# Cross attention of a deep block: split-precision products, transposed queries, shares scaled on VectorE

## What is computed

```python
def cross_attention(h, mm, wq, wk, wv, wo):
    q = (h @ wq).reshape(B, S, XA_HEADS, XA_HEAD_DIM)
    k = (mm @ wk).reshape(B, M, XA_HEADS, XA_HEAD_DIM)
    v = (mm @ wv).reshape(B, M, XA_HEADS, XA_HEAD_DIM)
    s = jnp.einsum('bshd,bmhd->bhsm', q, k) * (XA_HEAD_DIM ** -0.5)
    p = jax.nn.softmax(s, axis=-1)
    o = jnp.einsum('bhsm,bmhd->bshd', p, v).reshape(B, S, D_MODEL)
    return o @ wo
```

## Time and profile before

| | |
|---|---|
| median of 3 runs | 1783.58 us (1782.58 to 1783.75) |
| profiled execution | 1782.28 us, of which 1780.5 us lie between first and last instruction |
| PE busy | 97% of the span |
| DVE, ACT, POOL busy | 62%, 50%, 10% |
| mean granted PE clock | 0.995 of 2.4 GHz |

### The profile page before, as it was taken

How to read it: one execution, slowest core, us unless ns; L and a number is a source line. 1 busy time by engine, 2 the same in 40 slices (tenths; PEclk the granted TensorE clock), 3 DMA queues, 4 the chain that set the end, 5 groups by cost and what they waited for, 6 DMA issues and landing times.

```text
span 1780.5 us, 22807 instructions
## 1 busy us (share of the span) xinstructions
PE 1735.2 (97%) x9317; PEld 1473.0 (83%) x9317; DVE 1105.6 (62%) x1327; ACT 890.3 (50%) x1040; POOL 184.5 (10%) x142
## 2 busy tenths in 40 slices
PE   8989999999999999999999999999999999999997
PEld 6787999978878787999888878888888887888886
DVE  7867655568767754655556775565555667565554
ACT  6555544465556554544455445544445544654442
POOL 1100000014352241000021000000003000000000
PEclk9999999999999999999999999999999999999999
DMA  8426555555535526555565464465556456446551
GB/s 292 168 95 213 172 185 191 188 140 189 166 96 184 170 96 207 174 189 188 189 211 166 145 233 168 128 201 188 188 169 198 149 206 213 142 144 200 189 189 71
DMA packets 160791, 311.07 MB, mean 175 GB/s; under 512 B 5851, under 2 KB 53472, under 8 KB 159920
## 3 DMA queue, kind: packets, MB, share of 16 engines
q1 hardware_dynamic: 158512, 299.33, 50.7%
q0 software_dynamic: 2176, 10.29, 1.6%
HBM read 304.35 MB, written 5.24 MB: 174 GB/s over the span
## 4 chain that ended last, share of the span: by engine, by line
PE 83%; DVE 8%; ACT 5%; issue 2%; DMA 1%; POOL 1%; SPq 0%; DVEq 0%; ACTq 0%; POOLq 0%
PE ps L458 22%; PE ps L460 22%; PE ps L459 22%; PE ps L663 4%; PE ps L662 4%; PE ps L661 4%; PE ps L421 3%; DVE wlo L1447 3%; ACT whi L956 2%; DVE ps L1596 1%; PE ps L875 1%; ACT work L1053 1%; PE ps L891 1%; DMA raw<-in_a_w_qkv 1%; DMA sums<-st 1%
## 5 line engine op out<-in xcount | busy, mean ns | idle before, releaser
L1447 DVE TENSOR_TENSOR wlo<-raw,whi 128x2048 fp32r<-128x2048 f32 x279 | 643.3, 2309 | 435.8 <-ACT whi L956 426.6
L458 PE MATMUL ps<-whi,hT_hi 128*128 128x512 f32 x1936 | 765.4, 395 | 9.1 <-DVE hT_lo L1474 2.5
L460 PE MATMUL ps<-whi,hT_lo 128*128 128x512 f32 x1936 | 752.6, 389 | 0.0
L459 PE MATMUL ps<-wlo,hT_hi 128*128 128x512 f32 x1936 | 751.5, 388 | 0.0
L956 ACT ACTIVATE whi<-raw 128x2048 fp32r<-128x2048 f32 x279 | 533.8, 1914 | 361.8 <-PE ps L460 305.0
L458 PEld LDWEIGHTS ps<-whi,hT_hi 128*128 128x128 f32 x1936 | 364.4, 188 | 88.0 <-issue 10.8
L460 PEld LDWEIGHTS ps<-whi,hT_lo 128*128 128x128 f32 x1936 | 364.0, 188 | 76.2
L459 PEld LDWEIGHTS ps<-wlo,hT_hi 128*128 128x128 f32 x1936 | 364.7, 188 | 70.2
L661 PE MATMUL ps<-hT_hi,whi 128*128 128x256 f32 x640 | 182.8, 286 | 1.7 <-ACT work L1114 0.9
L662 PE MATMUL ps<-hT_lo,whi 128*128 128x256 f32 x640 | 181.5, 284 | 0.0
L663 PE MATMUL ps<-hT_hi,wlo 128*128 128x256 f32 x640 | 181.4, 283 | 0.0
(11 more groups left out here) (202 smaller groups left out, 1061.0 us busy)
## 6 DMA issues: line engine op xcount, KB each, us to landing
raw<-in_w_in SPq DMA_DIRECT2D x46, 1024.0 KB, 5.1
raw<-in_w SPq DMA_DIRECT2D x88, 512.0 KB, 4.6
raw<-in_m_w_up SPq DMA_DIRECT2D x32, 1024.0 KB, 5.2
raw<-in_m_w_down SPq DMA_DIRECT2D x32, 1024.0 KB, 4.8
raw<-in_kv_w SPq DMA_DIRECT2D x24, 1024.0 KB, 5.1
raw<-in_w SPq DMA_DIRECT2D x22, 1024.0 KB, 4.9
raw<-in_b_w_q SPq DMA_DIRECT2D x12, 1024.0 KB, 5.2
raw<-in_a_w_qkv SPq DMA_DIRECT2D x11, 1024.0 KB, 6.5
```

Of the source, the lines that this page charges most:

```text
L458: pe.matmul(acc, xh, wh, start=start and k == 0, stop=False)
L459: pe.matmul(acc, xh, wl, start=False, stop=False)
L460: ins = pe.matmul(acc, xl, wh, start=False, stop=stop and k == kc - 1)
L1447: vec.tensor_tensor(wlo[:, m % SPLIT, :], raw[:, m % RAW, :], whi[:, m % SPLIT, :], ALU.subtract).then_inc(*mark("lo_ready", ("lo", m)))
```

## The change

- The queries are projected by `up_chunk()`, transposed, without the row scale. ACT writes their rounded high part (`xq_hi`) and DVE the low part (`xq_lo`) straight from PSUM; `xa_turn_q` and the copies belonging to it go away. The row scale goes into the exponential instead: ACT takes it as `scale`, and DVE multiplies the maxima by its negative. DVE makes these two scale vectors after the row scale (two small products).
- The loaded keys and values are split into a high part (ACT, `memory_hi`, 128 x 2048) and a low part (DVE, `memory_lo`, the same size, in place). The keys' and the values' high parts and the keys' low part are written at the time of the product before (`w_o_2`), the values' low part in cross attention.
- Scores and values are three fp32r passes each in place of one fp32 matmul.
- The turned probabilities are split as well: `xp_hi` on ACT, `xp_lo` on DVE.
- DVE scales the exponentials itself (`xshare`: a reciprocal and two products of 128 x 256 a head); POOL does nothing here any more.
- On PE the scores of head 0 stand behind Q1, those of head 1 in the middle of Q2, the turn of head 0's probabilities behind Q2, values of head 0 and the turn of head 1 in the middle of Q3, and the values of head 1 and scores of heads 2 and 3 behind Q3. The rest keeps its place.

The core of the diff (declarations and walks shortened; eight leading blanks are cut):

```diff
-nat = sb("nat", [P, T, D])
+nat, nat_r = sb_twice("nat", [P, T, D])
...
-wide = sb("wide", [P, 2 * 3072])
+wide, wide_r = sb_twice("wide", [P, 2 * 3072])
...
-qn = pnf[:, 0:T * D].rearrange("p (t c) -> p t c", t=T)
-qT = pnf[:, T * D:T * D + KD * S].rearrange("p (k s) -> p k s", k=KD)
+q_hi, q_lo = [pn_r[:, KD * S * j:KD * S * (j + 1)].rearrange("p (k s) -> p k s", k=KD) for j in range(2)]
+k_hi = wide_r[:, 0:KD * S].rearrange("p (k s) -> p k s", k=KD)
+v_hi = wide_r[:, KD * S:KD * S + T * D].rearrange("p (t d) -> p t d", t=T)
+k_lo, v_lo = km_r.rearrange("p (k s) -> p k s", k=KD), vm_r.rearrange("p (t d) -> p t d", t=T)
...
-pxT = [pnf[:, 4608 + 512 * j:5120 + 512 * j].rearrange("p (m c) -> p m c", m=2) for j in range(2)]
+pT_hi = [pn_r[:, 4608 + 512 * j:5120 + 512 * j].rearrange("p (m c) -> p m c", m=2) for j in range(2)]
+pT_lo = [nat_r[:, 0, 512 * j:512 * j + 512].rearrange("p (m c) -> p m c", m=2) for j in range(2)]
...
         def xa_scores(h):
-            pe.wait_ge(*at("T free", uq_[h]))
+            pe.wait_ge(*at("q split", l, h))
             if h >= 2:
                 pe.wait_ge(*at("xexp", l, h - 2))
             elif h == 0:
-                pe.wait_ge(*at("merged", l, T - 1, 1))
-                pe.wait_ge(*at("mem back", l))
+                pe.wait_ge(*at("keys split", l))
             for t in range(T):
                 for k in range(2):
-                    ins = pe.matmul(ps[:, SC + h % 2, t * S:(t + 1) * S], qT[:, 2 * h + k, t * P:(t + 1) * P],
-                                    kmT[:, 2 * h + k, :], start=k == 0, stop=k == 1)
+                    acc = ps[:, SC + h % 2, t * S:(t + 1) * S]
+                    qh, ql = [q[:, 2 * h + k, t * P:(t + 1) * P] for q in (q_hi, q_lo)]
+                    kh, kl = [b[:, 2 * h + k, :] for b in (k_hi, k_lo)]
+                    pe.matmul(acc, qh, kh, start=k == 0, stop=False)
+                    pe.matmul(acc, qh, kl, start=False, stop=False)
+                    ins = pe.matmul(acc, ql, kh, start=False, stop=k == 1)
             ins.then_inc(*mark("scored", ("xscores", l, h)))
...
+            elif h == 0:
+                pe.wait_ge(*at("values split", l))
...
+                    acc = ps[:, OB + h % 2, j * S:(j + 1) * S]
+                    vh, vl = [b[:, k, d:d + P] for b in (v_hi, v_lo)]
+                    ph, pl = [b[h % 2][:, k, :] for b in (pT_hi, pT_lo)]
+                    pe.matmul(acc, vh, ph, start=k == 0, stop=False)
+                    pe.matmul(acc, vh, pl, start=False, stop=False)
+                    ins = pe.matmul(acc, vl, ph, start=False, stop=k == 1)
...
-        chunk(hT[0], tx[v + 1], early=lambda: x_half(v + 1, 1))
-        ch = c.ch
-        free = lambda t, half: ("acc free", ch - 1, t)
-        tile(hT[0], 0, ACCB, True, False, None, free, lambda: xa_scores(0), lambda: xa_turn_q(0))
-        xa_scores(1)
-        tile(hT[0], 4, ACCB, False, True, None, None, xa_middle, lambda: xa_turn_p(0))
-        c.ch += 1
-        xa_values(1)
-        xa_turn_q(1)
-        xa_scores(2)
-        xa_scores(3)
+        def xa_inside(n):
+            if n == 2:
+                xa_scores(1)
+            if n == 3:
+                xa_values(0)
+                xa_turn_p(1)
+
+        def xa_after(n):
+            if n == 1:
+                xa_scores(0)
+            if n == 2:
+                xa_turn_p(0)
+            if n == 3:
+                xa_values(1)
+                xa_scores(2)
+                xa_scores(3)
+
+        up_chunk(tx[v + 1], lambda: x_half(v + 1, 1), xa_after, 0, xa_inside)
+        up_chunk(None, None, xa_after, 2, xa_inside)
...
+        def memory_hi(to, loaded, name):
+            act.wait_ge(*at("mem back", l))
+            for t in range(T):
+                act.wait_ge(*at("merged", l, t, 1))
+            sc.activation(to, loaded, CP).then_inc(*mark("memory_hi", (name, l)))
+
+        tick()
+        tick()
+        c.ch += 1
+        memory_hi(k_hi, kmT, "keys hi")
+        tick()
+        memory_hi(v_hi, vm, "values hi")
+        tick()
+        c.ch += 1
+        x_half(v + 1, 0)
+
+        def xq_hi(h):
+            act.wait_ge(*at("acc", c.m - 1, h % 2, 0))
+            sc.activation(q_hi[:, 2 * h:2 * h + 2, :].rearrange("p k s -> p (k s)"), ps[:, ACC + h % 2, :], CP).then_inc(
+                *mark("q_hi", ("q hi", l, h)))
...
-            plain(pxT[h % 2].rearrange("p m c -> p (m c)"))
+            hi_of(pT_hi[h % 2].rearrange("p m c -> p (m c)"))
...
         begin(v + 1, junk2)
         tick()
-        out_of_acc(CP, lambda tt: qn[:, tt, 0:512], rs_of(v + 1))
-        tick()
-        xq_turn(0)
+        xq_hi(0)
+        xq_hi(1)
+        tick()
         xexps(0)
-        tick()
         xexps(1)
-        xp_turn(0)
+        tick()
+        xp_hi(0)
+        xq_hi(2)
         xo_hi(0)
-        xp_turn(1)
-        out_of_acc(CP, lambda tt: qn[:, tt, 512:1024], rs_of(v + 1))
+        xp_hi(1)
+        xq_hi(3)
+        c.ch += 2
         xo_hi(1)
-        xq_turn(1)
         tick()
         xexps(2)
         xexps(3)
-        xp_turn(2)
-        tick()
-        xp_turn(3)
+        xp_hi(2)
+        tick()
+        xp_hi(3)
         xo_hi(2)
         xo_hi(3)
...
+        def memory_lo(loaded, lo, hi, hi_key, key):
+            dve.wait_ge(*at(hi_key, l))
+            vec.tensor_tensor(lo, loaded, hi, ALU.subtract).then_inc(*mark("memory_lo", (key, l)))
+
+        tick()
+        tick()
+        add_chunk(v + 1, 0, c.m - 1)
+        memory_lo(kmT, k_lo, k_hi, "keys hi", "keys split")
+        tick()
+        last_to_x(v + 1)
+
+        def xq_lo(h):
+            dve.wait_ge(*at("q hi", l, h))
+            hi, lo = [b[:, 2 * h:2 * h + 2, :].rearrange("p k s -> p (k s)") for b in (q_hi, q_lo)]
+            vec.tensor_tensor(lo, ps[:, ACC + h % 2, :], hi, ALU.subtract).then_inc(*mark("q_split", ("q split", l, h)))
+            same[("acc free", c.ch, h % 2)] = ("q split", l, h)
+            c.ch += h % 2
+
+        def xp_lo(h):
+            c.tu = turned_at["xp", l, h]
+            if h >= 2:
+                dve.wait_ge(*at("xav", l, h - 2))
+            lo_of(pT_hi[h % 2].rearrange("p m c -> p (m c)"), pT_lo[h % 2].rearrange("p m c -> p (m c)"))
...
-            vec.tensor_scalar(mx[:, o:o + 2], big, -(256 ** -0.5), None, ALU.mult).then_inc(*mark("negmaxes", ("xnegmax", l, h)))
-
-        def xrec(h):
+            vec.tensor_tensor(mx[:, o:o + 2], big, rst[:, 6:8], ALU.mult).then_inc(*mark("negmaxes", ("xnegmax", l, h)))
+
+        def xshare(h):
             dve.wait_ge(*at("xexp", l, h))
-            vec.reciprocal(st[:, 16 + 2 * h:18 + 2 * h], st[:, 8 + 2 * h:10 + 2 * h]).then_inc(*mark("xrecs", ("xrec", l, h)))
+            rec = st[:, 16 + 2 * h:18 + 2 * h]
+            settle(dve, vec.reciprocal(rec, st[:, 8 + 2 * h:10 + 2 * h]), "xrecs", "xrec", l, h)
+            for t in range(T):
+                ins = vec.tensor_scalar(px[h % 2][:, t, :], px[h % 2][:, t, :], rec[:, t:t + 1], None, ALU.mult)
+            ins.then_inc(*mark("xshares", ("xshare", l, h)))
...
         begin(v + 1)
-        tick()
-        for n in range(2):
-            for t in range(T):
-                same[("qn", l, n, t)] = ("acc free", c.ch, t)
-            c.ch += 1
-        tick()
+        o = 2 * ((v + 1) % 2)
+        dve.wait_ge(*at("rs", v + 1))
+        vec.tensor_scalar(rst[:, 4:6], rst[:, o:o + T], 256 ** -0.5, None, ALU.mult)
+        settle(dve, vec.tensor_scalar(rst[:, 6:8], rst[:, o:o + T], -(256 ** -0.5), None, ALU.mult), "xroots", "xroot", l)
+        tick()
+        xq_lo(0)
+        xq_lo(1)
         xmax(0)
-        xrec(0)
+        xshare(0)
+        tick()
         xmax(1)
-        xrec(1)
-        dve.wait_ge(*at("xshare", l, 1))
-        tick()
+        xshare(1)
+        memory_lo(vm, v_lo, v_hi, "values hi", "values split")
+        tick()
+        xp_lo(0)
+        xq_lo(2)
         xo_lo(0)
+        xp_lo(1)
+        xq_lo(3)
         xo_lo(1)
         xmax(2)
         xmax(3)
-        xrec(2)
-        xrec(3)
-        dve.wait_ge(*at("xshare", l, 3))
-        tick()
-        tick()
+        xshare(2)
+        xshare(3)
+        tick()
+        xp_lo(2)
+        tick()
+        xp_lo(3)
         xo_lo(2)
         xo_lo(3)
...
-        for h in range(4):
-            pool.wait_ge(*at("xrec", l, h))
-            for t in range(T):
-                r = st[:, 16 + 2 * h + t:17 + 2 * h + t]
-                ins = g_.tensor_scalar(px[h % 2][:, t, :], px[h % 2][:, t, :], r, None, ALU.mult)
-            ins.then_inc(*mark("shares", ("xshare", l, h)))
```

More of the change, by code:

```diff
@@ L115, in sb, with sb_twice @@
             return ctx.enter_context(nc.sbuf_tensor(name, shape, dt))
+        def sb_twice(name, shape):
+            with nc.sbuf_tensor(name, shape, F32) as exact:
+                pass
+            return exact, sb(f"{name}_rounded", shape, F32R)
         raw = sb("raw", [P, RAW, TILE])
@@ L138, in build @@
         WORK = 14208
-        work = sb("work", [P, WORK])
+        work, work_r = sb_twice("work", [P, WORK])
```

(12 more changed lines are left out.)

17 lines of the change are left out of this document (3 added, 14 removed).

## The result

| | before | after |
|---|---|---|
| median (11 runs each) | 1782.58 us (1782.14 to 1784.21) | 1787.70 us (1786.52 to 1789.09) |
| profiled execution | 1782.28 us | 1787.56 us |
| span of the profiled execution | 1780.5 us | 1785.8 us |

The ratio is 1.0026 with an interval of 1.0018 to 1.0034: the change makes the kernel 0.26% slower, 5.1 us. The prediction had 5.3.

A forecast was written before the change was run, and what follows sets the result against it. PE, busy 97% of the span, was taken as the bound. Per layer -3.1 of PE work plus waits of 1.45, 2.6 and 0.5 gave +1.4, both +2.9; the clock added 2.4: 1787.6 us (1788.9 against the median), range 1782 to 1792.

The forecast's parts named there:

- the likeliest of the cases: The forecast's own case: PE waits for DVE and the clock falls at least once, 1786.5 to 1792.3 us, chance 0.55.
- PE's own work: PE's matmuls and transposes in cross attention if nothing waits: -3.1 us a layer, -6.3 for both.
- The term of scores and values: On PE, 12 three-pass matmuls, 1.44 us, in place of an fp32 group of 1.74, eight groups: -2.4 a layer.
- the old wait: PE's wait ahead of scores of heads 2 and 3 for the copy of the turned queries, 0.30 us, to go.
- The three waits: PE waiting for DVE: 1.45 us ahead of scores 0, 2.6 ahead of values 0, 0.5 ahead of values 3.
- one fall: PE's clock dropping to half behind the second wait, ahead of values 0, once in two layers: 2.9 us, less 0.5.
- the third wait: PE ahead of values 3, waiting for DVE's `xp_lo(3)`: 0.5 us, deducted again where a slower PE asks later.
- Waits, but the clock stays: Rival: the waits come in cross attention but PE's clock does not fall, +2.9, 1786.5 us; chance 0.27.
- The waits are half of mine: Rival: PE's waits for DVE's chain total 2.3 us a layer, -0.8 a layer, 1782 us; chance 0.10.
- No wait of weight: Rival: DVE and ACT keep ahead and the PE sum counts in full, 1777.3 us; chance 0.08.
- DVE is half idle: DVE has 26.6 us of work in a 51.7 us stretch; said to tell nothing about results being ready for PE.

The follow-up runs named there:

- the reordered kernel: The changed kernel with all its work in another order on DVE and ACT, splits wanted sooner put ahead of weight work: 1775.19 us, ratio 0.9957.
- with PE kept busy: The changed kernel with 22 unneeded transposes issued by PE in the gap ahead of values 0 of each layer: 1784.96 us, ratio 1.0012.

## Why the prediction was right

- **The sum.** +5.3 was forecast against the median, +5.1 measured, by the likeliest of the cases.
- **PE's own work.** Forecast -3.1 a layer; the reordered kernel shows -3.85. The term of scores and values was 0.30 a group and is 0.33, 0.2 of the missing 0.7. The rest I can only assign to the spacing behind switches between forms: the 51.70 us of the earlier trace rows are some 0.4 more than the groups times their spacing and the old wait (51.3), and I let that stand. One sentence had its base wrong: 1.74 against 1.44 makes the fp32 group 21% dearer, and the passes 17% cheaper; the sum took the right difference.
- **The three waits.** Forecast 1.45, 2.6 and 0.5 by start times; the profile writes 1.20, 2.67 and 0.46. Its idle time understates: from the slot of the next matmul (1094.28 + 0.12) to the actual start at 1095.76 are 1.36, and the first one is spaced 0.22 instead of 0.12, so 1.46. For the second and third, in the same way, 2.9 and 0.7. All three together 5.1 where I had 4.6.
- **The clock.** I took one fall at its full 2.9 in two layers, less 0.5, so 2.4. It was two falls of 1.56, so 3.1, in the profiled execution. The direction was right, and the number and the price of the falls were both wrong, in opposite directions: the low clock of the earlier trace rows lasted 5.8 us, that of the two new ones about 3.5. The price was also misread at its source. In the kernel before PE's next wait for ACT stands at 536.59, 13.72 us behind the gap, against 13.60 in kernels whose clock stayed at 1.00 there; that fall cost 0.1 us where it stood and not 2.9. Half the time at the lower clock is lost only where PE meets no other wait behind it, as in cross attention. One deduction has no ground: the third wait did not vanish, 0.46 in the changed kernel and 0.49 with PE kept busy.
- **Total of a layer.** -3.85 + 5.1 + 1.56 = +2.8, measured 2.87; forecast 1.4 + 1.2 = 2.6. That the sum came within 0.3 us owes something to luck: the saving and the waits were both too small, by 0.7 and 0.5. The mechanism, three waits for DVE and a clock that falls behind the second, is as forecast.
- **The rivals.** "Waits, but the clock stays" would be the kernel with PE kept busy, 1784.96, where 1786.5 was forecast: the larger saving takes off 1.4, the longer waits add 1.1, and the median of the kernel before is 1.0 lower beside these runs than the 1783.58 I started from. "The waits are half of mine" is out, with 5.1 us a layer where it had 2.3. "No wait of weight" was the potential: 1775.2 in the reordered kernel, 1777.3 forecast. "DVE is half idle" was a true sentence about the mean and said nothing of the moment.

What stays open: how much each of the five moves in the reordered kernel gives. Three of them were run by themselves (the values' subtraction, `xq_lo(0)` and `xp_lo(0)`), each with the others unmended; the maxima of head 1 ahead of O0 and the split of head 3 ahead of O3 were not. What sets whether a gap is followed by the lower clock is open as well: its length alone doesn't. Nor was it tried whether the 12.5 us hold with a different order of the heads on PE.

## What to carry to other kernels

Before work moves to an engine that is half idle, write down for each of its results the moment at which the bound engine asks for it, and what stands ahead in the queue that is wanted later: one weight subtraction of 2.2 us, needed 20 us later, made the difference between 0.26% slower and 0.14% faster. A wait removed ahead of another wait of the same chain gives nothing, and a queue emptied at one engine shows the one beside it; so mend the last wait first. A gap of PE costs about a quarter of a microsecond more than the idle time that the profile writes, and on top of that the low clock behind it, if PE is the bound there.
